# Attention steps spread over the plain projections' stage, with a product between the two parts of each step

## The reference, cut to what matters

```python
z = x @ w_in                    # q (1024) | k (256) | v (256) | rwkv (3328) | gates (2048)
A = windowed attention(q, k, v) # 16 heads of 64, 4 kv heads, window 128, blocks of 128, sinks, relative bias
B = rwkv7_time_mix(...)         # sequential state scan, 16 heads
mix = (sigmoid(gate_a) * (A @ w_branch_attn) + sigmoid(gate_b) * (B @ w_branch_rwkv)) @ w_out
h = layer_norm(alpha * x + mix)
y = layer_norm(alpha * h + peer(h))   # 128 experts out of 16384 per row
```

```python
s = q @ k.T * dh ** -0.5 + bias
m = maximum(s.max(-1), sink); p = exp(s - m)
o = (p / (p.sum(-1) + exp(sink - m))) @ v
```

## Time and profile before

| what | us |
|---|---|
| median of 3 runs | 4366.49 (4365.15 to 4375.88) |
| the profiled execution | 4375.91 |
| its span, first to last instruction | 4374.1 |
| TensorE busy in the span | 3791.0 |
| VectorE busy in the span | 3035.9 |
| early attention stage | 540 to 609 |
| late attention stage | 2105 to 2286 |

### The profile page before, as it was taken

How to read it: one execution, slowest core, us unless ns; L and a number is a source line. 1 busy time by engine, 2 the same in 40 slices (tenths; PEclk the granted TensorE clock), 3 DMA queues, 4 the chain that set the end, 5 groups by cost and what they waited for, 6 DMA issues and landing times. The chain is left out here.

```text
span 4374.1 us, 71420 instructions
## 1 busy us (share of the span) xinstructions
PE 3791.0 (87%) x28135; PEld 2533.3 (58%) x28135; DVE 3035.9 (69%) x5964; ACT 958.0 (22%) x2001; POOL 1802.3 (41%) x1489
## 2 busy tenths in 40 slices
PE   7976878799999888888778886668999999999998
PEld 6766765655555488787565464564544544455444
DVE  0454431678588658777777488876989788977777
ACT  1331230110133322222451013780000000000001
POOL 0007000057223034433225207735666566666665
PEclk9997879899999998898789997669999999999999
DMA  7542254389577467766549633459999999999998
GB/s 176 164 157 92 83 187 171 112 338 410 210 261 255 175 232 240 259 221 211 207 137 382 242 144 49 97 147 404 406 411 390 403 403 409 379 410 413 413 412 325
DMA packets 390906, 1152.47 MB, mean 263 GB/s; under 512 B 78174, under 2 KB 148387, under 8 KB 372995
## 3 DMA queue, kind: packets, MB, share of 16 engines
q0 software_dynamic: 207216, 687.87, 43.2%
q1 hardware_dynamic: 150628, 419.97, 25.9%
q10 hardware_dynamic: 32727, 40.05, 2.6%
HBM read 1044.67 MB, written 113.65 MB: 265 GB/s over the span
## 5 line engine op out<-in xcount | busy, mean ns | idle before, releaser
L2793 PE MATMUL x_vps<-l_c_v,x_w 128*128 128x512 f32 x1536 | 676.6, 602 | 38.4 <-DVE x_w L2842 38.4
L2785 PE MATMUL x_sps<-c_big,l_c_wo 128*128 128x384 f32 x2048 | 671.8, 490 | 26.8 <-DMA l_c_wo<-u_cols 23.6
L387 POOL DMA_INDIRECT l_w_ring<-u_rows,k_eidx x256 | 297.5, 1162 | 908.4 <-DVE l_w_dots L443 366.8
L387 POOL DMA_INDIRECT w_ring<-u_rows,k_eidx x384 | 478.2, 1245 | 402.2 <-DVE w_dots L443 238.5
L2785 PEld LDWEIGHTS x_sps<-c_big,l_c_wo 128*128 128x128 f32 x2048 | 391.5, 192 | 307.6 <-DMA l_c_wo<-u_cols 31.7
L460 DVE SCALAR_TENSOR_TENSOR l_c_share<-w_ring,w_wts,l_c_share 128x1024 f32<-128x1024 f32 x384 | 493.6, 1285 | 93.8 <-DMA w_ring<-v_rows,k_eidx 81.6
L2793 PEld LDWEIGHTS x_vps<-l_c_v,x_w 128*128 128x128 f32 x1536 | 296.4, 193 | 412.7 <-issue 361.4
L387 POOL DMA_INDIRECT w_ring<-v_rows,k_eidx x384 | 411.6, 1072 | 159.3 <-issue 109.6
L387 POOL DMA_INDIRECT l_w_ring<-v_rows,k_eidx x256 | 289.8, 1132 | 328.8 <-DVE l_w_yacc L460 264.8
L460 DVE SCALAR_TENSOR_TENSOR l_w_yacc<-l_w_ring,l_w_wts,l_w_yacc 128x1024 f32<-128x1024 f32 x256 | 328.9, 1285 | 28.0 <-DMA l_w_ring<-v_rows,k_eidx 19.4
L443 DVE CUSTOM_DVE_ANT_0 w_ring<-w_ring,w_h 128x1024 f32<-128x1024 f32 x256 | 302.9, 1224 | 38.4 <-DMA w_ring<-u_rows,k_eidx 26.2
(11 more groups left out here) (652 smaller groups left out, 6282.3 us busy)
## 6 DMA issues: line engine op xcount, KB each, us to landing
l_c_wo<-u_cols SPq DMA_DIRECT2D x64, 1024.0 KB, 9.4
l_c_v<-v_rows SPq DMA_DIRECT2D x32, 2048.0 KB
e_c_w<-w_tiles SPq DMA_DIRECT2D x54, 512.0 KB, 3.6
l_c_w<-w_tiles SPq DMA_DIRECT2D x54, 512.0 KB, 6.8
l_c_wo<-s_G SPq DMA_DIRECT2D x16, 1536.0 KB, 9.2
s_rw<-l_q_out SPq DMA_DIRECT2D x48, 384.0 KB, 5.2
s_G<-l_c_share ACTq DMA_DIRECT2D x8, 2048.0 KB, 7.9
s_zT<-l_pz ACTq DMA_DIRECT2D x30, 384.0 KB, 7.1
```

Of the source, the lines that this page charges most:

```text
L387: pool.indirect_dma_start(out=self.ring[:, r, :], out_offset=None, in_=self.A[table], in_offset=bass.IndirectOffsetOnAxis(ap=idx[:, s:s + ...
L2785: mm = pe.matmul(sps[n % 2][:, 0:ND * P], u[n % 4][:, k, :], hT[:, k, :], start=(k == 0), stop=(k == KT - 1))
L2793: mm = pe.matmul(vps[k][:, x * 512:(x + 1) * 512], w[:, e, k * P:(k + 1) * P], v[:, e, x * 512:(x + 1) * 512], start=(c == 0 and e == 0), ...
```

## The change

`project_plain` and `attend` become one stage, `project_attend`. Its first U0 tiles (16 early, 14 late) are projected as before, in units of one column group; keys, values, bias and q are then read back from memory by `attend_loads`, once v is stored. The rest of the units (14 early, 32 late) is laid out over slots: steps + 2, which is 10 early and 26 late. In slot s TensorE does sc(s) and pt(s-1), then one unit, then pv(s-1) and at(s-2), and in some slots one unit more (4 early, 6 late). ScalarE and VectorE follow the same order. Scores have one PSUM tile instead of two. The result of a step goes to `aT` in memory; it is loaded by `load_merge` in the scan's last turn, together with the first merge weights and gates and five of the eight tiles of `bT`, one more follows, and the last two stay where the scan made them. The values are turned in the new stage.

The small turns of the decode rows in the plain stage go; ScalarE stores them with one transfer per tile whose written elements lie 4 bytes each. The transfer of zeros to `G` is issued in the early merge after the step i = 0, which has no loads any more. The background plan is 10 groups over tiles 3 to 12, 14 groups over the 26 slots (four VectorE operations in a slot, eight in two of them, half before and half after the step's second part), and nothing in the place of attention; the other stages keep their numbers. `act` begins the choice at tile 2 instead of 5, and VectorE first waits for the sinks.

```diff
+def attend_loads(sp, A, pt, held, kv_in, att_in):
+    lo, at = (0, WIN) if pt.first else (pt.t0 - WIN, 0)
+    for name, t in (("kT", T_K), ("vT", T_V)):
+        sp.dma_start(held[name][:, :, at:], A["zT"][t:t + 2, :, lo:pt.t0 + pt.n].rearrange("t p c -> p t c")).then_inc(kv_in, 16)
+    src = bass.AP(A["tab"].tensor, WIN - 1, [[3 * WIN - 1, P], [P * 3 * WIN, NH], [1, 2 * WIN]])
+    sp.dma_start(held["bias"][:, :, :], src).then_inc(att_in, 16)
...
+def project_attend(nc, A, pt, bg, plan):
+
+    UN = 4
+    UNITS = NH // UN
+    NBUF = 2
+    STEPS_ = pt.NB * UNITS
+    SLOTS_ = STEPS_ + 2
...
+    U0 = LAST_Q + (4 if pt.first else 2)
+    left = [(u, g) for u in range(U0, N_PLAIN) for g in range(NG)]
+    more = len(left) - SLOTS_
+    assert 0 <= more <= SLOTS_
+    mid_of, end_of, o = [], [], 0
+    for s in range(SLOTS_):
+        mid_of.append(left[o:o + 1])
+        e = (s + 1) * more // SLOTS_ - s * more // SLOTS_
+        end_of.append(left[o + 1:o + 1 + e])
+        o += 1 + e
+    assert o == len(left)
...
+                if u == LAST_Q + 2:
+                    for j in range(2):
+                        sp.wait_ge(z_out[j], PER_Z * (LAST_Q // 2))
+                    if pt.first:
+                        sp.wait_ge(tab_out, 16)
+                    attend_loads(sp, A, pt, held, kv_in, att_in)
+                    for j in range(NBUF):
+                        load_q(j)
+                if u < U0:
                     bg.sp(sp, plan["groups"](u))
+                elif u < N_PLAIN:
+                    share = slot_groups * (u + 1 - U0) // (N_PLAIN - U0)
+                    bg.sp(sp, share - rows_of)
+                    rows_of = share
+                    while blocks < NBL and (u - U0 - 1) * NG >= (blocks - 1) * UNITS * len(left) // SLOTS_:
+                        sp.wait_ge(pe_done, PE.after(f"sc{UNITS * (blocks - NBUF + 1) - 1}"))
+                        load_q(blocks)
+                        blocks += 1
...
+            def unit(u, g):
+                v = NG * u + g
+                if g == 0:
+                    pe.wait_ge(w_in[u % 3], 16 * (u // 3) + 16)
+                if v >= 2:
+                    pe.wait_ge(z_sbuf, v - 1)
...
+            for s in range(SLOTS_):
+                if s < STEPS_:
+                    j, u = s // UNITS, s % UNITS
+                    if u == 0:
+                        pe.wait_ge(q_in[j % NBUF], 16 * (j // NBUF + 1))
...
+                        pe.wait_ge(dve_done, DV.after(f"s2_{s - 1}"))
...
+                if 0 <= m < STEPS_:
+                    pe.wait_ge(act_done, AC.after(f"e{UN - 1}_{m}"))
...
+                for u, g in mid_of[s]:
+                    unit(u, g)
+                if 0 <= m < STEPS_:
+                    j, u = m // UNITS, m % UNITS
+                    pe.wait_ge(act_done, AC.after(f"cp{m}"))
+                    if m >= 1:
+                        pe.wait_ge(dve_done, DV.after(f"on{m - 1}"))
...
+                for u, g in end_of[s]:
+                    unit(u, g)
...
+                if g < NG - 1:
+                    return
+                act.wait_ge(z_sbuf, v + 1)
                 for here, there in pt.spans:
                     act.dma_start(A["zT"][u, :, there], z[j][:, here]).then_inc(z_out[j], 16)
-                if pt.dec and u:
-                    natural(u - 1)
-                if u == 5:
+                if pt.dec:
+                    act.dma_start(A["zn"][:, u, :].rearrange("b p -> p b"), z[j][:, n:N], allow_slow_non_contiguous=True).then_inc(z_out[j], 16)
...
+                    act.activation(aTs[m % 2][:, :, :], atp[:, 0, :, :], ACT.Copy).then_inc(act_done, 1)
+                    act.wait_ge(act_done, AC.after(f"ac{m}"))
+                    there = slice(pt.t0 + j * WIN, pt.t0 + (j + 1) * WIN)
+                    act.dma_start(A["aT"][2 * u:2 * u + 2, :, there].rearrange("t p c -> p t c"), aTs[m % 2][:, :, :]).then_inc(at_out[m % 2], 16)
+                for u, g in end_of[s]:
+                    evacuate(u, g)
+                if sum(halves[:s + 1]) // 2 > sum(halves[:s]) // 2:
+                    bg.act(act, 1)
...
+            for s in range(SLOTS_):
+                if s < STEPS_:
...
+                    dve.wait_ge(pe_done, PE.after(f"sc{s}"))
+                    if s >= 2:
+                        dve.wait_ge(pe_done, PE.after(f"pt{s - 2}"))
+                    do(f"s1_{s}", V.scalar_tensor_tensor(Sx[s % 2][:, :, 0:WIN], scp[:, :, 0:WIN], pen[:, pt.b0 + j:pt.b0 + j + 1],
+                                                         bias[:, hs, 0:WIN], ALU.add, ALU.add))
+                    do(f"s2_{s}", V.tensor_tensor(Sx[s % 2][:, :, WIN:], scp[:, :, WIN:], bias[:, hs, WIN:], ALU.add))
...
+                bg.dve(dve, 2 * halves[s])
+                m = s - 1
+                if 0 <= m < STEPS_:
+                    dve.wait_ge(act_done, AC.after(f"es{m}"))
+                    do(f"den{m}", V.tensor_tensor(den[:, m, :], sums[:, m, :], es[:, m, :], ALU.add))
+                    do(f"rec{m}", V.reciprocal(den[:, m, :], den[:, m, :]))
...
+                bg.dve(dve, 2 * halves[s])
...
+            def load_merge(p):
+                first = A["sb_first"]
+                for x, name in enumerate(("wba_tiles", "wbr_tiles")):
+                    sp.dma_start(first["w"][x], A[name][0]).then_inc(merge_in, 16)
+                sp.dma_start(A["sb_aT"][:, :, 0:n], A["aT"][:, :, tokens].rearrange("t p c -> p t c")).then_inc(merge_in, 16)
+                for x, t in enumerate((T_GA, T_GB)):
+                    for here, there in pt.spans:
+                        sp.dma_start(first["g"][x][:, here], A["zT"][t, :, there]).then_inc(merge_in, 16)
+                for j in range(2):
+                    sp.wait_ge(y_out[j], 16 * len(range(j, p, 2)))
+                for k in LOADED:
+                    sp.dma_start(A["sb_bT"][:, k, 0:n], A["bT"][k, :, tokens]).then_inc(merge_in, 16)
+                return 3 + 2 * len(pt.spans) + len(LOADED)
...
+                if 0 < p < NPAIR - 1:
+                    store(p - 1)
                 if p:
-                    store(p - 1)
                     load_gb(p)
...
-                    n_att = load_attend(sp, A, pt, to_attend, kv_in, att_in)
+                    n_merge = load_merge(p)
             side.turn_back(sp)
-            store(NPAIR - 1)
-            sp.wait_ge(att_in, 16 * n_att)
-            for j in range(2):
-                sp.wait_ge(y_out[j], 16 * (NPAIR // 2))
+            sp.wait_ge(pe_chain, PC.after(ends, NPAIR - 1))
+            sp.dma_start(A["sb_bT"][:, BEHIND, 0:n], A["bT"][BEHIND, :, tokens]).then_inc(merge_in, 16)
+            sp.wait_ge(merge_in, 16 * (n_merge + 1))
...
-                    if i + x:
+                    if i:
                         sp.dma_start(w[j][x][:, :, :], A[name][i]).then_inc(w_in[j][x], 16)
...
-                for x, t in enumerate((T_GA, T_GB)):
+                for x, t in enumerate((T_GA, T_GB) if i else ()):
                     for here, there in pt.spans:
                         sp.dma_start(g[j][x][:, here], A["zT"][i + t, :, there]).then_inc(g_in[j], 16)
+                if i == 0:
+                    side.clear(sp)
...
+                    if i + x == 0:
+                        side.beside(pe)
...
+            side.place(act, src[0])
             for i in range(KT):
                 j, r = i % 2, i // 2
-                act.wait_ge(g_in[j], 32 * NSP * (r + 1))
+                if i:
+                    act.wait_ge(g_in[j], 32 * NSP * (r + j))
...
+    beside = {"groups": lambda u: 1 if 3 <= u < 13 else 0, "slot": lambda s: 2 if s % 13 == 6 else 1,
+              "pair": lambda p: 0 if p == NPAIR - 1 else 2 if p % 2 else 1, "turn": 3, "act": lambda c: 1 if c in (3, 7, 11) else 0,
+              "dve0": lambda c: 1, "dve1": lambda c: 1, "lead": 1, "group": lambda i: 1 if i % 2 else 2, "rest": 20}
```

More of the change, by code:

```diff
@@ new lines, in project_attend, with staged @@
+def project_attend(nc, A, pt, bg, plan):
[4 more added lines that the diff above has]
+    SLOTS_ = STEPS_ + 2
+    NBL, final, n = pt.NB, pt.last, pt.n
+    NG, GN, N = pt.ng, pt.gn, pt.N
+    LAST_Q = T_V + 2
+    U0 = LAST_Q + (4 if pt.first else 2)
[9 more added lines that the diff above has]
+    assert o == len(left)
+    def staged(front, mid, tail):
+        out = []
+        for s in range(SLOTS_):
+            for stage, d in ((front, 0), (mid, 1), (tail, 2)):
+                if 0 <= s - d < STEPS_:
+                    out += [x + str(s - d) for x in stage]
+        return out
+    PE = Steps(*staged(("sc",), ("pt", "pv"), ("at",)))
+    DV = Steps(*staged(("s1_", "s2_", "mx", "ms", "nm", "sd"), ("den", "rec", "on"), ()))
+    ac = []
+    for s in range(SLOTS_):
+        if 0 <= s - 1 < STEPS_:
+            ac.append(f"cp{s - 1}")
+        if s < STEPS_:
+            ac += [f"e{x}_{s}" for x in range(UN)] + [f"es{s}"]
+        if 0 <= s - 2:
+            ac.append(f"ac{s - 2}")
+    AC = Steps(*ac)
@@ L519, in project_plain @@
```

(23 more changed lines are left out.)

467 lines of the change are left out of this document (173 added, 294 removed).

## The result

The changed kernel takes 4470.59 us (median of 5 runs, 4463.31 to 4492.18), the kernel before 4369.99 beside it: a ratio of 1.0224, 95% interval 1.0203 to 1.0245. It is slower by 2.2%, where 1.7% faster was forecast; the time lies outside the range. The profiled execution took 4492.18 us, with a span of 4490.1, 116.0 more than the span before. It was the slowest of the five, so its stages add up to more than the 100.6 us between the medians.

What follows compares the result with a forecast made beforehand. The prediction took TensorE to bound the late projection and a chain the attention stages. Late -180 + 126 - 5 = -59 and early -68 + 37 + 15 = -16 gave -75, so 4291 us; range 4242 to 4350.

Steps and rivals of the forecast that it cites:

- The early plain stage, +37: Early projection with attention steps added: 37 us of steps, less small turns, plus a wait; +37 us (27 to 50).
- the element stores "at 0": Early plain stage: 4-byte stores of decode rows stay hidden, 32 ns a packet, 2 us per engine; 0 us.
- The second rival: Early part: element stores pace it, at 18 us a landing +102 us, 4393; chance 0.08.
- Late plain stage, +126: Late projection with 26 attention slots ends at 1275 us where it was 1149; +126 us (+94 to +193).
- The start: Late slots begin at 990 us, after uncontested loads of keys, values, table and q; bounds 979 and 1000.
- The slots: The 26 late slots take VectorE's time as the longer engine, 281 us, 10.8 us a slot.
- The first rival: Slots: the product does not cover the chain, 13 us a slot in place of 10.8, +57, 4348; chance 0.16.
- Late removal, -180: Late attention between scan and merge goes: 181 us there, about 1 us of barrier stays; -180 us.
- Early merge, +15: Early merge: second weights wait behind the zeros for G, TensorE idles 20 us; +15 us (0 to 25).
- Early removal, -68: Early attention stage goes, with 1 us of barrier left; -68 us.
- The third rival: Early merge: the zeroing is not in the way, as transfers of one queue share engines; -15, 4276; chance 0.10.
- The fourth rival: Attention hides behind waits VectorE had anyway, only TensorE's 91 us added late, 31 early; -112, 4254; chance 0.11.

Runs made afterwards that it cites:

- Experiment 1: The kernel before, with only the element stores of the decode rows of 30 tiles in place of the small turns: 4496.3 us, ratio 1.0263.
- 2: The changed kernel with element stores for tiles 0 to 13 only: 4421.7 us, ratio 1.0096.
- 3: The changed kernel without element stores, decode rows of tiles 0 to 13 turned by TensorE: 4367.6 us, ratio 0.9974.
- experiment 7: The changed kernel without element stores, with ScalarE's exponentials ahead of the tile's copy: 4353.9 us, ratio 0.9951.
- experiment 12: The changed kernel without element stores, exponentials ahead of the copy, zeros in the early scan, two background groups moved into the late pairs: 4314.4 us, ratio 0.9867.
- 5: The changed kernel without element stores, with the late bias table and q tiles 0 and 1 loaded earlier: 4361.2 us, ratio 0.9973.
- the base: The changed kernel without element stores, on which most later runs build: 4367.6 us, ratio 0.9974 to the kernel before.
- experiment 6: The changed kernel without element stores, with no background groups in the late slots, all 14 at the late merge's end: 4470.9 us.
- 8: The changed kernel without element stores, with no product between the two parts of a step: 4388.8 us, ratio 1.0027.
- 4: The changed kernel with the zeros for G issued in the early scan, not the early merge: 4460.6 us, ratio 1.0173.

## Why the prediction was wrong

**The early plain stage, +37 against +161.5: the step that failed.** The forecast took the element stores "at 0", by "32 ns a packet, 2 us for the 64 of an engine". Experiment 1 shows 140.8 us for them alone, 2 and 3 take 44 and 109 us out of the changed kernel. The division is right and the quantity is wrong, twice: the row is a mean over small and large packets (2269 of 2593 under 512 B, 130 over 8 KB), and a queue's share divided by its packets does not price a packet when it is the neighbours' packets that grow. 69 ns an element, the estimate of experiment 1, makes 4.4 us a tile for 64 elements on each of 16 engines, beside 27 ns x 64 = 1.7 us as booked; 4.7 were measured. The second rival, given 0.08, is what happened, and so is the sign that the prediction named, ScalarE waiting for `z` stores in the early part. Its price was short: it counted 16 tiles, and put the loss of all gain at 8.3 us each. 15 took 7.9, but the stores also held up the loads ahead of the slots (38.3 us of waiting in place of 8.7), and the 16 stores of the other tiles cost 44 us more. The Trainium skill, "DMA: Bandwidth & Descriptors", Rules for kernel authors, has the rule behind it (one descriptor per element); the trace agrees, with 28194 packets for 21 such stores (21504 elements) and their neighbours. Whether the engine reads, modifies and writes, as its Specifications say, no run here shows.

With this term at its forecast value the time would have been 4470.6 - 103 = 4367.6: still 77 above 4291. The early stage is then 52 us longer than before, 15 more than the 37; experiment 7 gives back 5.7 of them, and the rest was not taken apart.

**Late plain stage, +126 against +165.7.** Two terms of it were too small. *The start*, 157 us into the stage, was 176.4. The forecast priced the loads "uncontested" from the earlier trace rows, though it read 1.03 at 410 GB/s in the earlier trace rows. They were issued on time, 136.8 us after the stage's start beside 134 in the forecast, but the table landed after 37.7 us, not 12.7:

```profile
L515 SPq DMA_DIRECT2D l_a_bias<-s_tab x1: 469/469/469, 1082.9 to 1082.9; - x1
...
DMA to landing us min/median/max: 37.7/37.7/37.7
```

Fetches kept coming beside them: 5 MB of new loads under full engines have to be paid at 410 GB/s, and so has each group ahead of them; taking two away gave back the 20 us (experiment 12, where the table landed after 15.8 us), another order nothing (5). *The slots*, 10.8 us, were 11.8 (11.6 in the base), which with the stage's end makes the other 21 us. The forecast took "the longer engine". TensorE's own work is 10.5 (experiment 6), VectorE's alone was put at 10.8 and not measured by itself; together they give 11.6. Each waits for the other now and then, in the base TensorE for exponentials (17.4 us) and for the scores to be read (7.5), VectorE for the values' product (15.7). The first rival, the product does not cover the chain at 13 us a slot, is not what happened: the product covers the copy, and without it the slots take 12.1 (8).

**Late removal, -180 against -170.6.** From the scan's last operation to merge's first product it is as forecast, 1.1 us, but the scan's last turn takes 7 us more, at a granted clock of 0.53 in place of 0.73 (more of it at the lower of the two levels, 1.2 GHz). The windows after and before:

```profile
2336.00:2395.00 59.00, 45.75 (x484) 37.22 (x479) 29.36 (x70) 7.44 (x15) 1.52 (x1) 0.53 0.43 155
```
```profile
2053.00:2105.00 52.00, 38.72 (x489) 32.06 (x485) 28.67 (x70) 9.29 (x17) 0.94 (x1) 0.73 0.43 133
```

In six other kernels the clock was between 0.56 and 0.76, and this stretch differed by 14 us between the kernel before and that of experiment 1, whose code there is the same. So it is not shown to belong to the change; the cause stays open. The late merge's +6.6 (forecast up to +5 for one more group) comes back in every kernel with the new stage that keeps its groups (204.5 to 209.7 us in place of 198.8); it and the pairs' +0.5 (-5) were not taken apart.

**Early merge, +15: right. Early removal, -68: not contradicted.** +14.4, with a gap of 20.4 us where 20 was forecast; and 16 us of this stage back when the zeros move (4). The third rival falls. The early -64 in place of -68 is within what this stretch differs by with the same code (310.9 and 291.5 us before the change).

**The fourth rival**, attention hidden altogether, falls with the slots.

The mechanism claimed for the change, filling attention's waits with products, works, for little: in the base the two plain stages grow by 211 us and the stretches that held attention shrink by 244. Without its element stores the change is worth 0.3%, and 1.3% with the exponentials, the zeros and two groups put elsewhere.

## What to carry to other kernels

Count the separate pieces of a transfer before its bytes, and judge them by what the other queues' packets then take, not by their own queue's share. A load added to a stretch in which the DMA engines are full cost its bytes at the full rate here wherever it stood in the queue; only fewer bytes there helped. When two engines both want about nine tenths of a slot, do not take the longer of them for its length: here it was 11.6 us, where TensorE's own work is 10.5 and VectorE's was put at 10.8.

## What the runs showed of the hardware

1024 elements of 4 bytes on one queue made 512 KB loads on another take 13.5 us in place of 3.6, and the engines' packets of about 4 KB 601 ns in place of 198. ScalarE's issues grew too: most took 0.5 us, some up to 11.7 (a store of the same tile to `zT`; at most 4.4 in the kernel before), and in that time the engine did nothing else. A load of q held SyncE for up to 22.8 us in the late part, and for 22.3 in the base, which has no element stores.
